# Attention scores from split queries and keys, and compression columns laid out contiguously, in a float32 transformer kernel

## The reference

```python
def compress_blocks(kv, pe, w1, w2):
    ...
    sub = kv.reshape(b, g, n_sub, CMP_STRIDE, d)
    blocks = jnp.concatenate([sub[:, :, r:r + n_cmp] for r in range(ratio)], axis=3)
    blocks = (blocks + pe).reshape(b, g, n_cmp, CMP_LEN * d)
    return jax.nn.silu(blocks @ w1) @ w2
```

```python
def _mla_branch(x, w_in, q_norm, w_q_up, kv_norm, w_kv_up, w_out):
    ...
    q = (_rmsnorm(cq, q_norm) @ w_q_up).reshape(B, S, MLA_HEADS, MLA_NOPE_DIM + MLA_ROPE_DIM)
    kv = (_rmsnorm(ckv, kv_norm) @ w_kv_up).reshape(B, S, MLA_HEADS, MLA_NOPE_DIM + MLA_V_DIM)
    ...
    q_full = jnp.concatenate([q[..., :MLA_NOPE_DIM], q_rope], axis=-1)
    k_full = jnp.concatenate(
        [kv[..., :MLA_NOPE_DIM],
         jnp.broadcast_to(k_rope[:, :, None, :], (B, S, MLA_HEADS, MLA_ROPE_DIM))], axis=-1)
    v = kv[..., MLA_NOPE_DIM:]
    scale = (MLA_NOPE_DIM + MLA_ROPE_DIM) ** -0.5
    o = _dense_causal(q_full, k_full, v, scale).reshape(B, S, MLA_WIDTH)
    return (o * jax.nn.silu(gate)) @ w_out
```

## Time and profile before

| | |
|---|---|
| median of three runs | 1799.76 us |
| the profiled execution | 1799.32 us, of which its span 1797.4 us |
| instructions in the trace | 24794 |
| TensorE products (PE) | 1779.4 us busy, 9830 products |
| TensorE loads (PEld) | 1433.7 us |
| VectorE (DVE) | 912.3 us |
| ScalarE (ACT) | 791.3 us |
| GpSimd (POOL) | 636.5 us |
| DMA | 82 GB/s on average over the span |

### The profile page before, as it was taken

One profiled execution on the slowest core, in us unless ns is written; L12 is line 12 of the kernel. 1 busy time (PEld: TensorE's weight loads), 2 busy tenths in 40 slices (PEclk: granted clock), 3 DMA queues, 4 the chain that ended last, 5 costly groups with the idle time before them and its releaser, 6 DMA issues.

```text
span 1797.4 us, 24794 instructions
## 1 busy us (share of the span) xinstructions
PE 1779.4 (99%) x9830; PEld 1433.7 (80%) x9830; DVE 912.3 (51%) x2017; ACT 791.3 (44%) x1713; POOL 636.5 (35%) x390
## 2 busy tenths in 40 slices
PE   9999999999999999999999999999999999999997
PEld 6787877788988888889876798888877777887676
DVE  4558588563211101134778267674744243567764
ACT  5334355453321322234567445553354344446662
POOL 5534421154444453434322433224342324332222
PEclk9999999999999999999999999999999999999999
DMA  5322311153433332324222232113422322431211
GB/s 171 100 71 71 95 48 36 36 158 99 119 94 106 90 110 82 94 77 115 62 45 71 94 98 77 54 59 84 117 71 58 83 71 78 109 68 34 59 58 71
DMA packets 215173, 147.91 MB, mean 82 GB/s; under 512 B 51969, under 2 KB 197393, under 8 KB 215058
## 3 DMA queue, kind: packets, MB, share of 16 engines
q1 hardware_dynamic: 210736, 137.10, 27.3%
q10 hardware_dynamic: 4322, 9.24, 1.5%
HBM read 144.22 MB, written 2.10 MB: 81 GB/s over the span
## 4 chain that ended last, share of the span: by engine, by line
PE 92%; DVE 5%; ACT 2%; issue 0%; DMA 0%; POOL 0%; SPq 0%; DVEq 0%; ACTq 0%
PE PS L392 25%; PE PS L393 24%; PE PS L394 24%; PE PS L480 6%; PE PS L541 6%; PE PS L565 4%; PE PS L733 1%; DVE PS L1539 1%; ACT X L1072 1%; DVE X L1542 1%; DVE PS L1558 1%; PE PS L954 1%; PE PS L933 1%; PE PS L754 0%; ACT P L1090 0%
## 5 line engine op out<-in xcount | busy, mean ns | idle before, releaser
L2140 POOL TENSOR_TENSOR Wl<-Wr,Wh 128x1024 fp32r<-128x1024 f32 (+5 forms) x385 | 635.8, 1671 | 1127.2 <-ACT Wh L1013 1127.0
L392 PE MATMUL PS<-XTl,Wh 128*128 128x512 f32 (+1 forms) x1096 | 412.9, 377 | 1.0 <-DVE OBl L1574 0.8
L394 PE MATMUL PS<-XTh,Wh 128*128 128x512 f32 (+1 forms) x1096 | 408.2, 372 | 0.0
L393 PE MATMUL PS<-XTh,Wl 128*128 128x512 f32 (+1 forms) x1096 | 408.0, 372 | 0.0
L1013 ACT CAST Wh<-Wr 128x1024 fp32r<-128x1024 f32 (+5 forms) x292 | 268.2, 938 | 183.6 <-PE PS L394 137.7
L392 PEld LDWEIGHTS PS<-XTl,Wh 128*128 128x128 f32 x1096 | 206.5, 188 | 45.6 <-issue 9.7
L394 PEld LDWEIGHTS PS<-XTh,Wh 128*128 128x128 f32 x1096 | 206.4, 188 | 36.4
L393 PEld LDWEIGHTS PS<-XTh,Wl 128*128 128x128 f32 x1096 | 206.6, 188 | 34.5
L392 PE MATMUL PS<-Wl,XTh 128*128 128x512 f32 (+2 forms) x608 | 227.1, 374 | 1.2 <-POOL Wl L2140 0.8
L394 PE MATMUL PS<-Wh,XTh 128*128 128x512 f32 (+2 forms) x608 | 224.1, 369 | 0.0
L393 PE MATMUL PS<-Wh,XTl 128*128 128x512 f32 (+2 forms) x608 | 224.0, 368 | 0.0
(11 more groups left out here) (323 smaller groups left out, 2549.4 us busy)
## 6 DMA issues: line engine op xcount, KB each, us to landing
Wr<-in_w_in SPq DMA_DIRECT2D x38, 512.0 KB, 3.8
Wr<-in_fox_w_in SPq DMA_DIRECT2D x32, 512.0 KB, 4.1
Wr<-in_w_ffn_gate SPq DMA_DIRECT2D x22, 512.0 KB, 3.9
Wr<-in_w_ffn_up SPq DMA_DIRECT2D x22, 512.0 KB, 3.9
Wr<-in_w_ffn_down SPq DMA_DIRECT2D x22, 512.0 KB, 3.6
Wr<-in_swa_w_in SPq DMA_DIRECT2D x20, 512.0 KB, 3.9
Wr<-in_mla_w_in SPq DMA_DIRECT2D x16, 512.0 KB, 4.2
Wr<-in_mla_w_out SPq DMA_DIRECT2D x16, 512.0 KB, 3.4
```

The lines of the kernel that those rows point to most:

```text
L392: pe.matmul(o, l[0], r[1], start=start, stop=False)
L393: pe.matmul(o, l[1], r[0], start=False, stop=False)
L394: return pe.matmul(o, l[0], r[0], start=False, stop=stop)
L2140: ins = raw.tensor_tensor(l[:, cs], r[:, cs], h[:, cs].bitcast(F), sub)
```

## The change

Two things are changed that don't depend on each other.

**Compression's blocks.** KXh and KXl hold the same 560 values in another order: column 70 r + q instead of 8 q + r. The two instructions that write them read KF with a stride of eight columns and write in sequence by rows of 70; the 96 products take 69 columns that lie side by side.

**The scores without position.** QT and KT become pairs of a high and a low tile. ScalarE writes the high part of Q (with the scale, as before); VectorE writes the high part of K by its copy, which now rounds, then the low part of K, waits for ScalarE's Q and writes the low part of Q (bank times 96^-0.5 minus high part). In place of one float32 product over KT and QT, `scores` issues three with rounded operands: K low with Q high, K high with Q low, K high with Q high; then the rope product as before. The scores wait for VectorE's low part of Q instead of ScalarE's QT, and the bank of the queries' projection is given back by VectorE. In `prep` the keys' projection goes first.

```diff
--- before.py
+++ after.py
@@ -253,7 +253,7 @@
         with ExitStack() as cm:
             CQ, CK = splits(cm, "CQ", [128, 3, T]), splits(cm, "CK", [128, 2, T])
             m_GT = alloc(cm, "GT", [128, 8, T])
-            m_QT, m_KT = alloc(cm, "QT", [128, T]), alloc(cm, "KT", [128, T])
+            m_QT, m_KT = splits(cm, "QT", [128, T]), splits(cm, "KT", [128, T])
             QRT, KRT = alloc(cm, "QRT", [128, 8, T]), alloc(cm, "KRT", [128, T])
             m_V = alloc(cm, "V", [128, NT, D])
             with ExitStack() as c1:
@@ -669,7 +669,7 @@
                     b = open_banks[f"h{j}"]
                     e.wait_ge(weight_lo.at(i), *free(b), by_dve.at("kx", j))
                     for l in range(8):
-                        lhs = [KX[j][u][:, l0 + l:l0 + l + 545:8] for u in range(2)]
+                        lhs = [KX[j][u][:, 70 * l + l0 // 8:70 * l + l0 // 8 + 69] for u in range(2)]
                         ins = mm3(PS[b][0:69, 0:128], lhs, part(i, l, 128), l0 + l == 0, l0 + l == 15)
                     if l0 == 8:
                         ins.then_inc(*done(psum_full, "ch", j))
@@ -853,8 +853,8 @@
 
                 def prep(x):
                     hs = (2 * x, 2 * x + 1)
-                    proj_T((s, "pq", x), [(w_q[:, :, h, 0:64], 64 * j) for j, h in enumerate(hs)], CQ, c_ready, (by_act, (s, "pq", x)))
                     proj_T((s, "pk", x), [(w_kv[:, :, h, 0:64], 64 * j) for j, h in enumerate(hs)], CK, c_ready, (by_dve, (s, "pk", x)))
+                    proj_T((s, "pq", x), [(w_q[:, :, h, 0:64], 64 * j) for j, h in enumerate(hs)], CQ, c_ready, (by_dve, (s, "pq", x)))
 
                 for f in range(3):
                     job(f"g{f}")
@@ -879,8 +879,8 @@
                     give(b, (by_act, (s, "qt", c)), (by_dve, (s, "qt", c)))
 
 
-                def nope(u, i, n):
-                    return m_QT[half(u), tile(i)], m_KT[half(u), 0:n]
+                def nope(q, k):
+                    return lambda u, i, n: (m_QT[q][half(u), tile(i)], m_KT[k][half(u), 0:n])
 
                 def turned_part(x):
                     def operands(u, i, n):
@@ -895,7 +895,8 @@
                     elif kind == "prep":
                         prep(x)
                     elif kind == "score":
-                        scores(s, x, [(nope, paired), (turned_part(x), paired)], [by_act.at(s, "pq", x), by_dve.at(s, "pk", x), by_dve.at(s, "ckr"), by_act.at(s, "qt", 3), by_dve.at(s, "qt", 3)])
+                        scores(s, x, [(nope(0, 1), paired), (nope(1, 0), paired), (nope(0, 0), paired), (turned_part(x), paired)],
+                               [by_dve.at(s, "pq", x), by_dve.at(s, "pk", x), by_dve.at(s, "ckr"), by_act.at(s, "qt", 3), by_dve.at(s, "qt", 3)])
                     elif kind == "turn":
                         turn(s, x, P)
                     elif kind == "value":
@@ -1197,7 +1198,7 @@
                     for u in range(2):
                         act.copy(KF[64 * u:64 * u + 64, 280:536], bank["c", j][64:128, u:512:2]).then_inc(*by_act.next("c_in", j))
                     e.wait_ge(by_dve.at("pf", j), by_act.now())
-                    high(KX[j][0][:, :], KF[:, :], "kx_hi", j)
+                    high(KX[j][0].rearrange("p (r q) -> p r q", r=8), KF.rearrange("p (q r) -> p r q", r=8), "kx_hi", j)
                 elif name in ("ck8", "cv8"):
                     j = int(name == "cv8")
                     after(psum_full, "ch", j)
@@ -1363,7 +1364,7 @@
                     after(psum_full, s, "pq", x)
                     if x:
                         after(scores_full, s, x - 1, 1, 3)
-                    act.mul(m_QT[:, :], bank[s, "pq", x][:, :], scale).then_inc(*by_act.next(s, "pq", x))
+                    act.mul(m_QT[0][:, :], bank[s, "pq", x][:, :], scale).then_inc(*by_act.next(s, "pq", x))
 
                 job("v0")
                 job("g3")
@@ -1716,7 +1717,7 @@
                         for u in range(2):
                             copy(KF[64 * u:64 * u + 64, 280 * g + 264:280 * g + 280], bank["pf", j][64 * g:64 * g + 64, u:32:2], "pf", j)
                     e.wait_ge(by_act.at("kx_hi", j), by_dve.now())
-                    low(KX[j][1][:, :], KF[:, :], KX[j][0][:, :], "kx", j)
+                    low(KX[j][1].rearrange("p (r q) -> p r q", r=8), KF.rearrange("p (q r) -> p r q", r=8), KX[j][0].rearrange("p (r q) -> p r q", r=8), "kx", j)
                 elif name in ("ca", "cb"):
                     j = int(name == "cb")
                     e.wait_ge(psum_full.at("ct", j))
@@ -1960,7 +1961,11 @@
                     e.wait_ge(psum_full.at(s, "pk", x))
                     if x:
                         e.wait_ge(scores_full.at(s, x - 1, 1, 3))
-                    copy(m_KT[:, :], bank[s, "pk", x][:, :], s, "pk", x)
+                    copy(m_KT[0][:, :], bank[s, "pk", x][:, :], s, "pk_hi", x)
+                    e.wait_ge(by_dve.now())
+                    low(m_KT[1][:, :], bank[s, "pk", x][:, :], m_KT[0][:, :], s, "pk", x)
+                    e.wait_ge(by_act.at(s, "pq", x))
+                    ve.scalar_tensor_tensor(m_QT[1][:, :], bank[s, "pq", x][:, :], 96.0 ** -0.5, m_QT[0][:, :].bitcast(F), mult, sub).then_inc(*by_dve.next(s, "pq", x))
 
                 job("v0")
                 job("g3")
```

## The result

Over 20 executions each the changed kernel takes 1802.52 us (median, 1799.94 to 1804.65) and the kernel before 1799.78 us. The ratio is 1.0015, 95% interval [1.0009, 1.0022]: **2.7 us slower**, clear of zero and still under 0.2%. The forecast was 1799.2 us, with a range of 1793.0 to 1805.5 that holds the time; the sign of the move was wrong.

What follows compares the result with a forecast made beforehand. TensorE, busy 99% of the span, was taken as the bound. Compression -6.1 us and scores +5.5 us gave -0.6 on the profiled 1799.32 us; with the runs' median 0.44 higher, 1799.2 us, range 1793.0 to 1805.5.

Steps and rivals of the forecast that it cites:

- the gain of the columns: Compression's 96 products: steps of 0.068 us instead of 0.132 with contiguous columns, a gain of 6.1 us.
- stride rival: Compression's 96 products: their own 128 columns are the bound, not the stride; nothing gained there, 1805.3 us, chance 0.12.
- the scores, pair by pair: Latent attention: three products gain 0.22 us per pair, but new waits make it 2.75 us lost per layer, 5.5 in both.
- the last two rivals: Scores: loads of the same row half don't hide, 1817.7 us, chance 0.03; two heads don't run side by side, 1829.8, 0.05.
- the prediction's 105 ns: Scores: the time one stationary operand load per row half was taken to occupy on TensorE.
- step one: Compression: shorter jobs make nothing wait; next Z and weights are ready in time, with 2 us in hand.
- the upper bound that I had named: Compression's two copies that make KX, 0.66 and 0.74 us: the stride there costs nothing, to double; cost taken as 0.
- step two: TensorE, clock 1.00 in all stretches read: removed work is gained in full, unless a wait replaces it; new waits cost in full.
- the waits don't come: Latent attention's scores: no new waits, so every pair gains 0.22 us; 1790.2 us, chance 0.10.

Runs made afterwards that it cites:

- e10: Kernel before with the new column layout, KF filled in that order and m3 ahead of the compression's last products, scores unchanged: 1792.70 us.
- e8: e3 with Q's low part made and used later, waits split per product, one rounding less ahead of Q, and KF filled in the new order: 1791.51 us.
- e9: Changed kernel with GpSimd almost idle beside the compression, making only 32 columns of six weight pieces' low halves: 1799.89 us.
- e1: Kernel before with the compression's new column layout alone, scores still one float32 product: 1796.28 us.
- e3: Changed kernel with projection m3 moved ahead of the compression's last products at the linear attention's last level: 1800.21 us.
- e4: Changed kernel with unread products on other data put into two new TensorE waits, at L699 and pair 2's scores: 1799.96 us.
- e11: e8 with the second half of the value projection moved from behind pair 4's prep to between pair 2's prep and its turn: 1790.88 us.

## Why the prediction was right and wrong

**Right: the gain of the columns.** Forecast 0.068 us a step and 139 ns a load, measured 0.064 and 142; forecast 6.1 us for the 96 products, 6.6 in e10. The stride rival is out.

**Right: the scores, pair by pair.** What each pair of mla0 adds to the difference (rope product's start), forecast and measured:

| pair | 0 | 1 | 2 | 3 | 4 | 5 | 6 | 7 | sum |
|---|---|---|---|---|---|---|---|---|---|
| forecast | 0.98 | -0.22 | 1.67 | -0.08 | -0.22 | -0.08 | 0.08 | 0.62 | 2.75 |
| measured | 1.09 | -0.25 | 1.64 | -0.11 | -0.22 | -0.14 | 0.06 | 0.60 | 2.67 |

A first part without a wait lasts 2.11 us, forecast 2.14. The 3 times 1280 columns of one head are 1.60 us at 2.4 GHz, and its twelve loads at the prediction's 105 ns would add 1.26. So loads of the same row half do hide, and the two heads do run side by side with rounded operands; the last two rivals are out. The 96 products show the first on all 128 rows: they start 0.064 us apart beside loads of 142 ns. The Trainium skill's rule that spoke against the change (TensorE: Matmul & The Clock Gate, "Part 3: Packing small matmuls"), that a load overlaps a running matmul only if it is in another row group, does not describe what these rows show. One thing was missed in the change's favour: 0.48 us per layer come back behind pair 7, where the turn before had to wait for its probabilities. The turn and the gate projection behind it, before and after:

```profile
982.71 2.57 PE L480 MATMUL PS<-CST,P 128*128 128x128 f32 x20
985.38 0.47 PE L392 MATMUL PS<-XTl,Wh 128*128 128x512 f32 x1
```

```profile
984.27 2.40 PE L480 MATMUL PS<-CST,P 128*128 128x128 f32 x20
986.46 0.47 PE L392 MATMUL PS<-XTl,Wh 128*128 128x512 f32 x1
```

The turn spans 2.67 us before (982.71 to 985.38) and 2.19 after: a loss just ahead of a place that was waiting anyway is partly free.

**Wrong, step one: "Does anything wait when the jobs end 3 us earlier each?"** I looked at the first Z and at the weights, and answered no. The copies went to the upper bound that I had named (nothing, to double) while I took nothing. At 1.28 and 1.26 us they put VectorE back far enough that, with GpSimd beside it, 0.60 us was lost before the first stretch and 0.8 waiting for Z; without either of the two nothing is lost there (e8, e9). And I never worked out VectorE's whole cycle per level against the new length of a stretch; I took for Z the 0.42 us of the earlier trace rows, which VectorE had reached only while GpSimd paused, although EX already took up to 0.97 beside GpSimd before. With stretches half as long the two nearly always meet, VectorE needs 4.50 to 4.88 us where TensorE needs 4.25, and L699, with next to nothing left ahead of it, shows the debt: 1.83 us. Shown by e1, e3 and e9. The forecast had -6.1 us for this place; the rows, without the fall of the clock, have -3.3. That alone turns the sign.

**Wrong, step two: "a new wait costs in full", and no more.** The clock was 1.00 wherever TensorE worked before (its waits behind the start were 1.1 us at most), and I left it there although the change, by my own sum, puts idle times of more than a microsecond into it. A wait of 1.2 to 1.8 us can cost as much again through the clock: 1.6 and 1.5 us in the profiled execution. Shown by e4. The fastest of the 20 executions, 1799.94 us at a clock of 0.999, lies 0.7 us above the forecast. In the profiled execution the end moved by +4.5 us against a forecast of -0.6, a miss of 5.1: the two falls are 3.1 of it, the waits and slower copies of step one 2.8, the start 0.6; the layers, which lost 4.4 without a fall against 5.5 forecast, and 0.3 between them give 1.4 back.

The rival *the waits don't come* (1790.2) was rightly held to be unlikely. It is also what the kernel could have been: with the waits taken out, e8 reaches 1791.51 and e11 1790.88.

## What to carry to other kernels

When a stretch of the bounding engine gets shorter, hold the whole cycle of the engine that works beside it against the new length, at the durations that it has when its neighbours run, and follow its debt to the first place without cover. Where a new wait on TensorE of the size seen here (1.2 to 1.8 us) is put into a busy stretch, give it a second term: it costs its idle time, and in some executions as much again through the clock behind it. And split a wait by what each product reads: an operand that is needed last can be made last, and a bank that is freed late should be handed out late.

## What was unexpected of the hardware

- The stationary operand's 32-byte stride cost 86 ns per load (228 to 142 ns, 69 columns) and half of the rate of the products.
- A cast of 128x560 on ScalarE that reads with a stride of 8 elements takes 1.28 us for 0.66, VectorE's difference with it 1.26 for 0.74, and copies of 64x256 that write with a stride of 70 elements 0.63 for 0.37 to 0.42.
- VectorE's 128x256 operations with both inputs in SBUF take 0.42 us alone, up to 0.97 beside GpSimd's operations of 128x256, and 1.61 beside one of 128x1024, ending 0.28 us after it.
- Idle stretches of 1.2 to 1.8 us on TensorE were followed, not each time, by some 3.4 us at the 1.2 GHz level; seven or four products on other data in their place kept 2.4 GHz.
